# A two-block transformer on one core: the last 256 columns of gates and ups of each feed-forward multiplied as one job of 512 columns

## What is computed

```python
def swiglu(x, w_gate, w_up, w_down):
    return (jax.nn.silu(x @ w_gate) * (x @ w_up)) @ w_down

    for l in range(DEPTH):
        x = layer_norm_2(ALPHA * x + 0.5 * swiglu(x, ffn1_gate[l], ffn1_up[l], ffn1_down[l]),
                         ln1_g[l], ln1_b[l])
...
        x = layer_norm_2(ALPHA * x + 0.5 * swiglu(x, ffn2_gate[l], ffn2_up[l], ffn2_down[l]),
                         ln3_g[l], ln3_b[l])
```

## Time and profile before

| | before |
|---|---|
| median of 3 runs | 1870.49 us |
| their range | 1869.71 to 1872.28 us |
| the profiled execution's own time | 1868.49 us |
| its span, first to last instruction | 1866.7 us |
| TensorE busy, granted clock | 98% of the span, 0.996 of full speed |
| VectorE, ScalarE, GpSimd busy | 70%, 54%, 6% |
| read from the chip's memory | 424 MB, 228 GB/s over the span |

### The profile page before, as it was taken

One profiled execution on the slowest core, in us unless ns is written; L12 is line 12 of the kernel. 1 busy time (PEld: TensorE's weight loads), 2 busy tenths in 40 slices (PEclk: granted clock), 3 DMA queues, 4 the chain that ended last, 5 costly groups with the idle time before them and its releaser, 6 DMA issues.

```text
span 1866.7 us, 21829 instructions
## 1 busy us (share of the span) xinstructions
PE 1830.5 (98%) x9112; PEld 1531.4 (82%) x9112; DVE 1302.3 (70%) x1333; ACT 1013.4 (54%) x1083; POOL 107.6 (6%) x101
## 2 busy tenths in 40 slices
PE   7999999999999999999999999999999999999998
PEld 6788888887978888887888888888888888888886
DVE  4579999987779899897554677655465546875544
ACT  6447777775646777774443374544344434735431
POOL 1020000001010000000000300100010003020000
PEclk9999999999999999999999999999999999999999
DMA  9447999996446999996555653655565556346541
GB/s 341 153 163 265 357 370 356 359 363 224 137 135 225 359 361 346 375 363 226 188 193 167 195 181 106 207 191 176 191 206 190 176 192 203 134 141 211 190 169 57
DMA packets 220170, 426.57 MB, mean 229 GB/s; under 512 B 7560, under 2 KB 28304, under 8 KB 220064
## 3 DMA queue, kind: packets, MB, share of 16 engines
q1 hardware_dynamic: 214256, 406.93, 63.3%
q0 software_dynamic: 5808, 18.17, 3.2%
HBM read 424.01 MB, written 1.06 MB: 228 GB/s over the span
## 4 chain that ended last, share of the span: by engine, by line
PE 92%; DVE 4%; ACT 2%; DMA 1%; issue 0%; POOL 0%; DVEq 0%; SPq 0%
PE ps L485 26%; PE ps L477 25%; PE ps L480 25%; DVE Wlo L426 2%; PE ps L596 2%; PE ps L469 1%; PE ps L470 1%; PE ps L2526 1%; PE ps L1306 1%; PE ps L1619 1%; PE ps L576 1%; PE ps L575 1%; PE ps L574 1%; ACT Whi L414 1%; PE ps L2427 1%; PE ps L2022 1%
## 5 line engine op out<-in xcount | busy, mean ns | idle before, releaser
L426 DVE TENSOR_TENSOR Wlo<-raw,Whi 128x2048 fp32r<-128x2048 f32 (+2 forms) x387 | 865.6, 2243 | 409.9 <-ACT Whi L414 409.2
L414 ACT ACTIVATE Whi<-raw 128x2048 fp32r<-128x2048 f32 (+2 forms) x393 | 736.0, 1878 | 474.9 <-PE ps L485 469.7
L485 PE MATMUL ps<-Whi,XTl 128*128 128x512 f32 (+2 forms) x1496 | 549.5, 377 | 0.0
L477 PE MATMUL ps<-Whi,XTh 128*128 128x512 f32 (+2 forms) x1368 | 521.0, 381 | 9.4 <-DVE Wlo L426 8.0
L480 PE MATMUL ps<-Wlo,XTh 128*128 128x512 f32 (+2 forms) x1368 | 514.8, 376 | 0.0
L485 PEld LDWEIGHTS ps<-Whi,XTl 128*128 128x128 f32 x1496 | 280.7, 189 | 50.6
L477 PEld LDWEIGHTS ps<-Whi,XTh 128*128 128x128 f32 x1368 | 258.4, 189 | 57.5 <-DVE Wlo L426 8.0
L480 PEld LDWEIGHTS ps<-Wlo,XTh 128*128 128x128 f32 x1368 | 258.4, 189 | 44.6 <-issue 0.3
L477 PE MATMUL ps<-Whi,hTh 128*128 128x512 f32 x352 | 137.8, 391 | 0.0
L485 PE MATMUL ps<-Whi,hTl 128*128 128x512 f32 x352 | 137.1, 390 | 0.0
L480 PE MATMUL ps<-Wlo,hTh 128*128 128x512 f32 x352 | 137.1, 389 | 0.0
(11 more groups left out here) (350 smaller groups left out, 1998.7 us busy)
## 6 DMA issues: line engine op xcount, KB each, us to landing
raw<-in_moe_w_gate SPq DMA_DIRECT2D x64, 1024.0 KB, 5.7
raw<-in_moe_w_up SPq DMA_DIRECT2D x64, 1024.0 KB, 6.4
raw<-in_moe_w_down SPq DMA_DIRECT2D x64, 1024.0 KB, 6.0
raw<-in_ffn_gate SPq DMA_DIRECT2D x44, 1024.0 KB, 5.1
raw<-in_ffn_up SPq DMA_DIRECT2D x44, 1024.0 KB, 5.1
raw<-in_ffn_down SPq DMA_DIRECT2D x40, 1024.0 KB, 5.0
raw<-in_w_in SPq DMA_DIRECT2D x18, 1024.0 KB, 5.2
raw<-in_a_w_in SPq DMA_DIRECT2D x10, 1024.0 KB, 13.2
```

Of the source, the lines that this page charges most:

```text
L414: act.activation(Whi[:, i % NS, 0:m * n], raw[:, i % NR, 0:m * n], ACT.Copy).then_inc(w_rounded, tick(w_rounded, "rounded", i))
L426: dve.tensor_tensor(Wlo[:, i % NR, 0:m * n], raw[:, i % NR, 0:m * n], h.bitcast(f32), ALU.subtract).then_inc(w_rest, tick(w_rest, "rest", i))
L477: pe.matmul(o, xh(k, t), h[:, q, :], start=k == first, stop=False)
L485: x = pe.matmul(o, xl(k, t), h[:, q, :], start=False, stop=k == end)
```

## The change

The last 256 columns of a layer's gate weights and the last 256 of its up weights are laid side by side on the host, as one tensor of 512 columns for each feed-forward. Chunk 5 becomes one job, `fboth`, of two units; the gate's products are the first 256 columns of its bank and the up's the last 256. Its gate activation and its gate-times-up both read that bank, and VectorE alone frees it. The transposes of chunk 4 now stand behind the job's first unit.

```diff
@@ plan_ffn
-        for c, b in enumerate(CH):
+        for c, b in enumerate(CH[:5]):
             plan_cols(("fgate", a, l, c), A[f"{a}_gate_2"][l], *b)
             plan_cols(("fup", a, l, c), A[f"{a}_up_2"][l], *b)
+        plan_cols(("fboth", a, l), A[f"{a}_both"][l], 0, 512)
@@ ffn_pe
-        for c in range(6):
+        for c in range(5):
...
+        for z in job_pe(pe, ("fboth", a, l), xt_h, xt_l, ready):
+            if z == 0:
+                turn(4)
         for z in job_pe(pe, ("fdown", a, l, 0), ht_h, ht_l, h_ready):
             if z == 0:
                 turn(5)
@@ ffn_act
-            n, name = CH[c][1] - CH[c][0], ("fgate", a, l, c)
+            n, name = CH[c][1] - CH[c][0], ("fgate", a, l, c) if c < 5 else ("fboth", a, l)
...
-                free(act_done, name, t)
+                if c < 5:
+                    free(act_done, name, t)
...
-            for z in job_act(act, ("fup", a, l, c), None):
+            for z in job_act(act, ("fup", a, l, c), None) if c < 5 else ():
                 pass
@@ ffn_dve
-            n, name = CH[c][1] - CH[c][0], ("fup", a, l, c)
+            n, name = CH[c][1] - CH[c][0], ("fup", a, l, c) if c < 5 else ("fboth", a, l)
...
-                dve.scalar_tensor_tensor(hd[:, t, 0:n], sg[:, t, 0:n], 0.5, PS[b][:, 0:n], ALU.mult,
+                src = PS[b][:, 0:n] if c < 5 else PS[b][:, 512 - n:512]
+                dve.scalar_tensor_tensor(hd[:, t, 0:n], sg[:, t, 0:n], 0.5, src, ALU.mult,
                                          ALU.mult).then_inc(dve_done, tick(dve_done, "hd", a, l, c, t))
...
-            for z in job_dve(dve, ("fgate", a, l, c), None, skew=c == 0):
+            for z in job_dve(dve, ("fgate", a, l, c), None, skew=c == 0) if c < 5 else ():
...
             for z in job_dve(dve, name, up):
-                pass
+                if c == 5 and z == 0:
+                    turn(4)
@@ kernel
+    for f in ("ffn1", "ffn2"):
+        inputs[f"{f}_both"] = np.concatenate([inputs[f"{f}_{k}_2"][:, :, 2560:] for k in ("gate", "up")], axis=2)
```

## The result

The changed kernel takes 1868.59 us in the median of 11 runs (1864.72 to 1870.13), the kernel before 1873.25 us in 11 runs alongside (1868.86 to 1878.72). The ratio is 0.9977, interval 0.9966 to 0.9988, which is a gain of 4.3 us. The forecast was 1868.0 us, 0.6 under the measured median, and a gain of 2.5 us, a ratio of 0.9987, just inside the interval. A second comparison (experiment 2) gave 0.9981 (0.9972 to 0.9990). So the gain lies at the bound of 0.2% that I had set for no change, and neither interval says on which side.

What follows compares the result with a forecast made beforehand. TensorE's matmul issue was taken as the bound in the feed-forwards. Saving 0.63 us in each of four, 2.5 us in all (2.4 to 2.6), from a median of 1870.49 gave 1868.0 us, 1866.8 to 1869.5 with scatter.

Steps and rivals of the forecast that it cites:

- What bounds the kernel: In the feed-forwards, TensorE's time to issue matmuls sets the pace and other engines wait; busy 1830.5 of 1866.7 us.
- What the change removes: In each feed-forward, 48 matmuls and 48 weight loads go, 0.0133 us per pair of matmuls joined, 0.64 us.
- The transposes: Chunk 4's eight transposes inside the job cost 0.87 us before and after; the stretch becomes 11.75 us (11.73 to 11.78).
- What it adds and moves: Later activation, rounding and product at the chunk's end, VectorE's order, banks and transfers: all claimed to cost nothing.
- T + 1.2: VectorE's last gate-times-up claimed to end 1.2 us after T, the end of the joined job's last matmul.
- the rounding: ScalarE's rounding of weights, queued behind the gate activation, starts some 0.3 us later; 11 us of slack, no cost.
- The cover I named: The down projection's first 24 matmuls, 5.44 us, hide the later product; without them about 0.6 us more per feed-forward.
- The sum: Whole kernel: median 1870.49 us less 2.5 us gives 1868.0 us, 0.13% less, counting as no change.
- A: Joined job runs at its weight loads' pace, 0.189 us, saving 9.8 us in all: 1860.7 us; chance 0.02.
- B: Chunk 5's transposes wait for VectorE's product and the kernel ends slower, 1875.8 us; chance 0.02, weaker form 0.01 more.
- C: New weights in memory slow the expert stages' transfers, adding 7.4 us: 1875.4 us; chance 0.02.
- D: Saving not reached, through hand-overs in the joined job or reading errors: 0 to 1.5 us saved, about 1869.8; chance 0.08.

Runs made afterwards that it cites:

- experiment 2: The changed kernel, unchanged, run again beside the kernel before on one chip: 1868.86 us, 0.9981 of the kernel before.
- experiments 3 and 5: Changed kernel, matmuls cut into 256 columns except each row tile's first and last: joined job only, 1871.98 us (0.9997); with five up jobs too, 1883.36 us (1.0071).
- experiment 7: Changed kernel with chunk 5's four transposes moved ahead of the down projection's first unit: 1873.50 us, 1.0014 of the kernel before.
- experiment 12: Changed kernel with three idle 512-column matmuls ahead of each down projection, restoring about the old timing: 1873.52 us, 1.0002 of the kernel before.
- experiment 4: Changed kernel with the joined job's matmuls cut into four of 128 columns: 1910.11 us, 1.0193 of the kernel before.
- experiments 6 and 7: Chunk 5's transposes moved ahead of the down projection's first unit, in the kernel before (1873.33 us, 1.0011) and in the changed one (1873.50 us, 1.0014).

## Why the prediction was right, and what it missed

**What bounds the kernel**: right. The 2.47 us saved in the four feed-forwards came out of TensorE's stream, and no other engine's time set the end of a stretch.

**What the change removes**: right. 13.3 ns for each matmul less was 0.64 us for each feed-forward; experiments 3 and 5 add matmuls back and pay 13 to 14 ns for each. The isolated gap of the Trainium skill ("TensorE: Matmul & The Clock Gate", section "Back-to-back issue gap"), 2.5 ns of fixed part, would have made it an estimated 0.5 us in all; no run here agrees with it.

**The transposes**: the term was 0.87 us, and what came was 11.78 to 11.81 against 11.75 predicted, 0.03 to 0.06 more. My bound was 11.78, and the first stretch lies above it. That the four saved 2.47 us all the same, and not 2.3, is the 0.03 us less in each first unit of the down projection, which I had not counted: two small errors that nearly cancel.

**What it adds and moves**: T + 1.2 was T + 1.04, the rounding 0.2 later where I said 0.3. Banks, transfers and VectorE's order cost nothing. The cover I named was the right one, and experiment 7 shows what it hid: 0.9 us each, 0.4 more than in the kernel before, where I had said 0.6.

**The sum**: the term for the matmuls was right, and the sum had no term for the clock. I took the saving off the median as if the granted clock stayed as it was, and counted scatter as something that only widens the range. The clock's falls behind TensorE's stands are worth 1.2 to 2 us each, they are in the trace of before as a window at 0.72, and I read the tenths of the slices, all 9, and left them. The changed kernel had fewer of them, which is likely where some 1.1 us beyond the 2.5 comes from; that the change causes this through its timing is argued from experiment 12 and not shown. The forecast of no measurable change holds in one comparison and just fails in the other, at -0.19% and -0.23% with a bound of 0.2%. That the median came within 0.6 us of 1868.0 is partly luck: the 1870.49 that I subtracted from was the median of three runs, and that of eleven is 1873.25. The 0.09 for faster was too low for a gain that was two thirds of the bound before any surprise.

**The rivals**: A did not come; its price for the loads' pace, 0.189 us, was also wrong, since a record is not a pace (0.112 in experiment 4). B did not come; experiments 6 and 7 took its cover away and found a stand of under 1 us. The 0.03 for slower was also added up wrong, since B and C had 0.02 each. C did not come: the first expert stage's pieces agree within 0.1 us in all traces. D did not come: the stretches lost 0.57 to 0.59 us each.

**The faster version**: the changed kernel with 12 idle matmuls, 1865.3 and 1865.6 us, on the same chip, 0.9968 of before both times.

## What to carry to other kernels

Where TensorE's stream is the bound, the price of an edit is read from the distance between starts at both widths, and a narrow job is worth joining for its fixed part alone: little at 256 columns, and much at 128, where a matmul took 0.112 us and not 0.067. A result that moves from the middle of a job to its end needs the next unit's work as cover: look for it before, and keep it. And when a gain is near the scatter, find the scatter's places first, by cutting two traces at the same landmarks and comparing piece by piece; here one number of idle matmuls, 18 or 12, was worth 1.6 us of the trace, against 2.5 for the change.

## What the runs showed of the hardware

Between 512 and 256 columns a matmul with its own weight load costs its columns at 2.4 GHz plus 13.3 ns (0.2267 and 0.1200 us); at 128 columns it costs 0.112 us, where the same sum gives 0.067, and at 32 columns about as much. A stop and restart of TensorE for 0.3 to 0.7 us costs 0.2 us more than the wait. Behind stands of 0.5 to 2.5 us the granted clock fell to its lower level in some executions and not in others of the same kernel, for 1.2 to 2 us of extra time; 100 runs of one kernel spanned 13 us, with mean clocks from 0.996 down to 0.990. And a fall need not stand beside a listed wait: in the execution of experiment 4 the first mixer's piece took 120.55 us and not 113.4, with clocks of 0.81 and 0.91. The list has no wait of TensorE from 1050 to 1190 us. The clock fell at 1092 us, amid matmuls of 280 and of 30 columns that this mixer has in every execution, and stayed at the lower level for 17 us, which I can't explain:

```profile
1080.00:1100.00 20.00, 20.00 (x113) 18.64 (x111) 10.96 (x18) 6.61 (x8) 0.00 (x0) 0.81 0.74 248
1100.00:1150.00 50.00, 50.00 (x258) 42.62 (x259) 33.93 (x61) 35.52 (x84) 0.89 (x1) 0.91 0.37 125
1092.30:1109.30 17.00, 17.00 (x79) 17.00 (x79) 3.76 (x5) 6.21 (x9) 0.00 (x0) 0.50 0.27 98
```
